# Moving the tile limits and the token table behind the first expert products in a routed mixture-of-experts kernel

## The reference

```python
group_logits = xf @ w_group
group_prob = softmax(group_logits)
g_idx = argmax(group_logits)                       # one of 4 groups
exp_logits = einsum('td,gde->tge', xf, w_expert)
sel = exp_logits of group g_idx
top_logit, top_j = top_k(sel, 2)                   # two experts of the group
weights = g_w[:, None] * softmax(top_logit)
...
a = einsum('td,edf->tef', x, w_gate)
b = einsum('td,edf->tef', x, w_up)
hid = silu(a) * b * combine[:, :, None]
y = einsum('tef,efd->td', hid, w_down)
```

## Time and profile before

| | |
|---|---|
| median of 3 runs | 768.46 us (765.98 to 769.75) |
| profiled execution, its time | 767.06 us |
| span of the profile | 765.2 us |
| PE busy | 646.9 us (85%) |
| DVE busy | 296.5 us (39%) |
| ACT busy | 132.4 us (17%) |
| POOL busy | 120.6 us (16%) |
| DMA moved | 291.11 MB, mean 380 GB/s |

### The profile page before, as it was taken

The page is one execution under the profiler, slowest core; times in us unless marked ns, Lnnn a source line. Parts: engine busy times, 40 slices in busy tenths (PEclk is TensorE's granted clock), DMA queues, the critical chain, the costliest instruction groups (busy, mean ns, idle before and its releaser), DMA issues.

```text
span 765.2 us, 12739 instructions
## 1 busy us (share of the span) xinstructions
PE 646.9 (85%) x4693; PEld 348.5 (46%) x4693; DVE 296.5 (39%) x721; ACT 132.4 (17%) x328; POOL 120.6 (16%) x194
## 2 busy tenths in 40 slices
PE   3899999999999999999844577899999997564685
PEld 3443343445796865554321232647655553222231
DVE  1215336765314644444221113666544443112123
ACT  3211134553116300000000000554000000000000
POOL 1000000001000033333312001010343333111010
PEclk9999999999999999999977689999999999777798
DMA  9999868949278799999999999999999999999996
GB/s 331 426 428 427 359 229 319 431 191 419 118 294 352 260 399 418 417 420 419 417 426 419 423 421 391 415 425 420 362 418 411 420 425 415 420 425 418 422 412 255
DMA packets 39577, 291.11 MB, mean 380 GB/s; under 512 B 7466, under 2 KB 8898, under 8 KB 20448
## 3 DMA queue, kind: packets, MB, share of 16 engines
q1 hardware_dynamic: 30112, 272.46, 86.2%
q0 software_dynamic: 7600, 12.81, 4.8%
q10 hardware_dynamic: 1808, 5.06, 1.7%
HBM read 284.68 MB, written 17.56 MB: 395 GB/s over the span
## 4 chain that ended last, share of the span: by engine, by line
PE 58%; DMA 26%; SPq 9%; DVE 4%; issue 2%; ACT 1%; DVEq 0%; POOLq 0%; POOL 0%
PE bank L1748 15%; PE bank L1449 8%; PE bank L1785 7%; DMA adas<-in_moe_w_in 6%; PE bank L1374 5%; DMA ring<-in_moe_w_in 4%; DMA cond_at<-in_moe_w_in 4%; PE bank L1548 4%; DMA ring<-in_ada_w 4%; DMA ring<-in_moe_w_out 4%; PE bank L1707 2%; PE bank L1556 2%; DMA adaw<-rows,gidx 2%; PE bank L1487 2%; PE bank L1508 2%
## 5 line engine op out<-in xcount | busy, mean ns | idle before, releaser
L1748 PE MATMUL bank<-ring,qkv 128*32 128x256 f32 (+1 forms) x1344 | 134.2, 423 | 39.4 <-DMA ring<-in_moe_w_in 25.0
L1748 PEld LDWEIGHTS bank<-ring,qkv 128*32 128x32 f32 (+1 forms) x1344 | 76.8, 133 | 82.4 <-issue 52.1
L1206 DVE COPY qkv<-bank 128x512 f32<-128x512 f32 x44 | 30.4, 691 | 200.8 <-PE bank L1707 200.8
L603 POOL DMA_INDIRECT results<-adaw,scur x46 | 47.2, 1026 | 249.9 <-DVE adaw L1229 216.3
L867 ACT ACTIVATE qkv<-bank 128x128 f32<-128x128 f32 x48 | 13.3, 277 | 408.5 <-PE bank L1748 408.5
L1785 PE MATMUL bank<-ring,qkv 128*32 128x512 f32 (+1 forms) x368 | 66.3, 609 | 4.6 <-DMA ring<-in_moe_w_out 4.6
L1449 PE MATMUL bank<-ring,hT 128*128 128x512 f32 x144 | 65.5, 610 | 1.3 <-DVE hT L947 1.3
L1748 PE MATMUL bank<-seventh,qkv 128*64 128x256 f32 (+1 forms) x224 | 35.5, 485 | 16.4 <-DMA ring<-in_moe_w_in 16.4
L593 POOL DMA_INDIRECT adaw<-rows,gcur x40 | 41.6, 1039 | 33.0 <-POOL gcur L590 27.8
L1449 PEld LDWEIGHTS bank<-ring,hT 128*128 128x128 f32 x144 | 27.3, 194 | 38.1 <-issue 36.9
L1748 PE MATMUL bank<-adaw,qkv 128*64 128x256 f32 (+1 forms) x256 | 36.6, 449 | 7.9 <-DMA adas<-in_moe_w_in 7.9
(11 more groups left out here) (260 smaller groups left out, 832.0 us busy)
## 6 DMA issues: line engine op xcount, KB each, us to landing
ring<-in_moe_w_in SPq DMA_DIRECT2D x37, 2048.0 KB, 19.9
ring<-in_moe_w_out SPq DMA_DIRECT2D x44, 1024.0 KB, 26.4
ring<-in_ada_w SPq DMA_DIRECT2D x14, 2048.0 KB, 14.8
adaw<-in_ada_w SPq DMA_DIRECT2D x10, 2048.0 KB, 15.2
adaw<-in_moe_w_in SPq DMA_DIRECT2D x8, 2048.0 KB, 22.6
seventh<-in_moe_w_in SPq DMA_DIRECT2D x8, 1792.0 KB, 24.9
xT<-in_moe_w_in SPq DMA_DIRECT2D x8, 1536.0 KB, 19.8
hT<-in_moe_w_out SPq DMA_DIRECT2D x10, 1024.0 KB, 25.4
```

Of the source, the lines that this page charges most:

```text
L603: pool.indirect_dma_start(res, bass.IndirectOffsetOnAxis(ap=scur[:, p, :], axis=0), yout[:, p], None, bounds_check=res_limit, oob_is_err=F ...
L1206: V.tensor_copy(xgT[:, p], bank[2][:, :]).then_inc(xgT_ready, 1)
L1748: last = T.matmul(bank[p][64 * a + m * h:64 * a + m * (h + 1), 0:2 * P], xk[:, k % 4, k // 4, m * h:m * (h + 1)], gate_up_of(b, k)[:, :, a ...
```

## The change

On PE, only the product that spreads the experts' order stays ahead of the rest of `first_rows`. The other four products (first place, capacity, places behind, extra tiles) go into a function `place_limits`, called behind the gate and up product of tile 0. The token table, which stood between the gate products of tiles 0 and 1, moves behind that of tile 1. DVE casts the experts' order first, as soon as its one product is there, and raises `over_ready` for it; its copy of the limits and all that follows now waits for `place_limits`. SP's first refill waits for the cast instead of `token_at`. Layer 1 is changed alike.

```diff
-                sp.wait_ge(slots_ready, l * 5 + 2)
+                sp.wait_ge(over_ready, l * 3 + 3)
                 refill_in(GATES)
...
                 dve.wait_ge(over_mm, l * 3 + 1)
-                dve.wait_ge(over_ready, l * 2 + 2)
+                V.tensor_copy(order_e[0:1, :], bank[2][0:1, 2 * NE:3 * NE]).then_inc(over_ready, 1)
+                dve.wait_ge(over_mm, l * 3 + 2)
                 order(V.tensor_copy(rt[:, 32:96], bank[2][:, 0:2 * NE]))
                 V.tensor_tensor(work, pos, rt[:, 64:96].unsqueeze(1).to_broadcast(shape), ALU.is_ge)
-                V.tensor_tensor(masked, pos, rt[:, 32:64].unsqueeze(1).to_broadcast(shape), ALU.add)
-                order(V.tensor_copy(order_e[0:1, :], bank[2][0:1, 2 * NE:3 * NE]))
-                dve.wait_ge(over_mm, l * 3 + 2)
+                order(V.tensor_tensor(masked, pos, rt[:, 32:64].unsqueeze(1).to_broadcast(shape), ALU.add))
...
-                pe.wait_ge(over_ready, l * 2 + 1)
-                for i in range(2):
-                    T.matmul(bank[2][:, i * NE:(i + 1) * NE], rt[0:NE, 156 + i:157 + i].to_broadcast([NE, P]), ident[0:NE, 0:NE],
-                             start=True, stop=True)
+                pe.wait_ge(over_ready, l * 3 + 1)
                 T.matmul(bank[2][:, 2 * NE:3 * NE], C("expert")[0:NE].to_broadcast([NE, P]), rt[0:NE, 192:224],
                          start=True, stop=True).then_inc(over_mm, 1)
-                T.matmul(bank[7][:, 128:128 + NE], rt[0:NE, 158:159].to_broadcast([NE, P]), ident[0:NE, 0:NE], start=True, stop=False)
-                pe.wait_ge(over_ready, l * 2 + 2)
-                T.matmul(bank[7][:, 128:128 + NE], rt[0:NE, 152:153].to_broadcast([NE, P]), C("later")[0:NE],
-                         start=False, stop=True).then_inc(over_mm, 1)
                 first_rows(0, (2, 3)).then_inc(tab_mm, 1)
                 first_rows(1, range(4)).then_inc(tab_mm, 1)
+
+                def place_limits():
+                    pe.wait_ge(over_ready, l * 3 + 3)
+                    for i in range(2):
+                        T.matmul(bank[2][:, i * NE:(i + 1) * NE], rt[0:NE, 156 + i:157 + i].to_broadcast([NE, P]),
+                                 ident[0:NE, 0:NE], start=True, stop=True)
+                    T.matmul(bank[7][:, 128:128 + NE], rt[0:NE, 158:159].to_broadcast([NE, P]), ident[0:NE, 0:NE],
+                             start=True, stop=False)
+                    T.matmul(bank[7][:, 128:128 + NE], rt[0:NE, 152:153].to_broadcast([NE, P]), C("later")[0:NE],
+                             start=False, stop=True).then_inc(over_mm, 1)
...
                 gate_up_mm(0, [0], range(HALF, KD)).then_inc(gu_mm, 1)
+                place_limits()
+                gate_up(1, 1, old=False)
                 token_table()
-                gate_up(1, 1, old=False)
                 hidden_T(0, 0, old=False)
```

More of the change, by code:

```diff
@@ L1121, in router @@
                 V.tensor_reduce(of_place, by_place, AX.X, ALU.add).then_inc(over_ready, 1)
-                dve.wait_ge(over_ready, l * 2 + 1)
+                dve.wait_ge(over_ready, l * 3 + 1)
                 order(V.tensor_tensor(excess, bank[3][0:NE, 0:1], rt[0:NE, 157:158], ALU.subtract))
```

## The result

The changed kernel takes 778.39 us in the median of four runs (776.68 to 783.45), the kernel before 767.67 (765.98 to 769.75). The ratio is 1.0138 with a 95% interval of 1.0104 to 1.0172: 8 to 13 us slower, 10.6 by the ratio. The forecast was 777.6 us. The profiled execution took 776.68 us with a span of 774.8, 9.6 more than before; the forecast for it was 776.2.

What follows compares the result with a forecast made beforehand. Token table, indices and tile 2's gather were taken to bound the path, with the transfer queue empty before rank 9. Two layers of 4.56 us make 9.1, on the 768.46 us median 777.6 us; range 772.5 to 782.0.

Steps and rivals of the forecast that it cites:

- Tile 0's gate product 1.01 us sooner: On PE, products taken from ahead of `first_rows` let it, ACT's copies and tile 0's gate product come 1.01 us sooner.
- `place_limits` costs 1.01 us behind it, DVE copies 1.12 us behind its start: Layer 0: eight PE records take 1.01 us from 262.65; DVE's copy of the limits can start at 263.77.
- 4.40 us of DVE work, 0.95 us of idle PE ahead of the table: DVE work from limits to `at_place`, without the cast, takes 4.40 us; tile 1's gate product leaves 0.95 us uncovered.
- Table 4.56 us later: Layer 0's token table on PE starts at 268.22 instead of 263.66, because DVE's work begins only behind tile 0's product.
- Gather 6.72 us in layer 0: The gather of tile 2's rows keeps its present time, issued after the indices and landing at 277.71.
- Turn and rank 9 +4.56 per layer: Tile 2's turn moves from 273.19 to 277.75 and rank 9's refill from 280.10 to 284.66; layer 1 shifts another 4.56 us.
- The shift passes to the end: The weight queue is empty ahead of rank 9 in both layers, so a later tile 2 lengthens the hole by as much.
- Early refills are worth nothing: Refills of ranks 7 and 8 start 1.0 and about 1.7 us sooner, without gain if the queue runs dry before rank 9.
- A floor under tile 2 of 2.0 us, PE idle about 2.5 us ahead of the turn: PE's down product ends near 275.2, so tile 2 turns at least 2.0 us later; PE then idles about 2.5 us.
- the short gather: Rival: a quick gather lets tile 2 turn at PE's floor, 2.0 us later per layer, giving 772.5 us; chance 0.12.
- The slow gather with the clock: Rival: an 8.1 us gather and PE at half clock add 2.9 us per layer, giving 783.4 us; chance 0.18.
- the kernel would not become slower: Rival: the queue absorbs the later tile 2 and only layer 0's earlier first refill counts, giving 767.5 us; chance 0.05.

Runs made afterwards that it cites:

- 9 fillers: Kernel before with only the token table moved behind tile 1's gate product, plus 14 unread products on PE, 9 ahead of tile 2's turn: +13.6 us, 1.0180.
- the two runs of one layer each: The change with limits and table moved late in layer 0 only, then layer 1 only, against the kernel before: +4.2 us (1.0063) and +5.9 us (1.0079).
- one experiment: Changed kernel with the token table again ahead of tile 1's gate product, only the limits late: +13.5 us against the kernel before, 1.0185.
- two runs here: Kernel before with `gate_rows` wholly behind tile 2's gate product, then half ahead and half behind with DVE copies reordered: +1.9 us (1.0021) and +3.1 us (1.0037).

## Why the prediction was right, point by point

- *Tile 0's gate product 1.01 us sooner.* It starts at +6.08 instead of +6.97: 0.89.
- *`place_limits` costs 1.01 us behind it, DVE copies 1.12 us behind its start.* 1.00 (261.26 to 262.26) and 1.11 (262.37).
- *4.40 us of DVE work, 0.95 us of idle PE ahead of the table.* 4.41 and 0.90.
- *Table 4.56 us later.* 4.68 and 4.67, since tile 0 came 0.89 and not 1.01 sooner.
- *Gather 6.72 us in layer 0.* 6.58, and 6.61 in layer 1: the nearest rows were the right price here. The other runs show how narrow that was: 2.4 to 3.0 us with only little beside the gather, 4.3 and 5.3 with the limits ahead of tile 0, 7.3 to 8.1 with the table late alone, 8.8 with 9 fillers.
- *Turn and rank 9 +4.56 per layer.* +4.54 and +4.66; +4.53 and +4.67. Sum 9.2 against 9.1.
- *The shift passes to the end.* Shown by the two runs of one layer each, and by the empty stretches of some 4 us (the forecast said 5 to 6).
- *Early refills are worth nothing.* Rank 8 was 1.6 us sooner, and the queue stood empty all the same. The down refill of rank 6 was mis-sized: 3.8 us later, not 2.8.
- *A floor under tile 2 of 2.0 us, PE idle about 2.5 us ahead of the turn.* Mis-sized: 1.51 us idle. The down product started as forecast (+20.32 against +20.27), but took 2.82 us instead of 1.94, so the floor was 3.0. PE's clock had fallen, which the forecast held possible only behind a gap longer than 2.27 us. The result table was slow too (2.20 instead of 1.46), which cost nothing: the down product had to wait for DVE's copy of the hidden rows (271.55 + 0.28 = 271.83) anyway. The gather covered the rest.

The nearness of the time, 778.39 against 777.6, is in part luck: the rise was 1.6 us more than the 9.1 of the sum, and the runs of before lay 0.8 us lower in the median than the 768.46 it was added to.

The rivals: the short gather came in one experiment, where the queue stood empty, with PE in the way. The Trainium skill's fit for a GpSimd DMA (DMA: Bandwidth & Descriptors, Anatomy of one DMA) gives 2.6 us for 128 rows of 2 KB, an estimate; the 2.4 to 3.0 measured there agree with it. It takes more bytes than moved, though: by the page of the profile GpSimd's queue (q0) moved 12.81 MB in all, on average at most 140 KB for each of the 92 gathers and scatters, not 262. Beside weight transfers the changed kernel's own gathers took 5.4 to 6.6 us, and there the row decided, not the fit. The slow gather with the clock is what the run with the late table alone shows: 7.3 to 8.1 us and `gate_rows` at half clock, 11.8 us in all. That the kernel would not become slower is out by the result, and by both runs of one layer. The sum of 9.2 lies inside the interval of 8 to 13 us, so the measured 10.6 asks for no further cause.

## What to carry to other kernels

Before moving a small product behind a large one, follow what it feeds: four products of 1 us in sum had 4.4 us of work on another engine behind them and a gather of 6.6 behind that, and the whole chain moved by what it lost in cover. A transfer allowed sooner gained nothing here, since the queue ran empty behind it all the same; look for the one release that ends the empty stretch and measure every edit by it. A gain ahead of it must then be followed for several tiles, since the next wait may take it back, as it did in two runs here.

## What the hardware showed unexpectedly

PE's granted clock fell to 0.50, 1.2 GHz, behind two short gaps, not one long one. In layer 0 of the changed kernel the gaps were 0.90 us ahead of 266.83 and 1.00 us ahead of 269.60; the stretches of one microsecond (PE busy, clock, DMA share, GB/s) show it:

```profile
268.00:269.00 1.00, 0.60 (x8) 1.00 0.92 382
269.00:270.00 1.00, 0.40 (x4) 1.00 1.09 459
270.00:271.00 1.00, 1.00 (x9) 0.65 1.15 490
271.00:272.00 1.00, 1.00 (x7) 0.50 0.95 410
272.00:273.00 1.00, 1.00 (x4) 0.50 0.99 426
```

In the kernel before, a single gap of 2.27 us had left it at 1.00, and in the changed kernel the later gap of 1.51 us did too. So the length of the gap just ahead does not tell whether the clock falls; what does was not settled. The second surprise is the spread of a gather of tiles 2 and 3, issued at the same line: 2.4 to 3.0 us where the weight queue stood empty, 4.3 to 9.7 in the other runs. In the steady state of the changed kernel the gathers of L593 took up to 11.0 us.
